# Scores of a prompt attention as float32r products over split keys, in place of float32 products over padded rows

## What is computed

```python
for l in range(DEPTH):
    fq, fk, fv, flf, mq, mckv, mkpe, sq, sk, sv = _mixer_inputs(_rmsnorm(xp, g_attn[l]), pos_p, *proj)
    o_a = _sweep(fq, fk, fv, True, jnp.cumsum(flf, axis=1))
    mk, mv = _mla_kv(mckv, mkpe, w_ukv[l])
    o_b = _sweep(mq, mk, mv, False)
    o_c = _swa_prompt(sq, sk, sv, rel_bias, swa_sinks[l])
    xp = xp + _merge(o_a, o_b, o_c, w_out[l])
    xp = xp + _mlp(_rmsnorm(xp, g_mlp[l]), w_up[l], w_down[l])
# in each attention: logits = jnp.einsum('bqhd,bkhd->bhqk', q, k) * scale, then softmax, then the product with v
```

## Time and profile before

| | |
|---|---|
| median of 3 runs | 2810.1 us (2809.98 to 2814.61) |
| profiled execution | 2807.96 us, span 2806.0 us |
| mean granted clock of PE | 0.989 |
| PE busy | 2695.5 us, 96% |
| DVE, ACT, POOL busy | 1698.6, 1054.8, 1050.4 us (61, 38, 37%) |
| chain that ended last | PE 86%, DVE 8%, ACT 2%, issue 2% |

### The profile page before, as it was taken

One profiled execution on the slowest core, in us unless ns is written; L12 is line 12 of the kernel. 1 busy time (PEld: TensorE's weight loads), 2 busy tenths in 40 slices (PEclk: granted clock), 3 DMA queues, 4 the chain that ended last, 5 costly groups with the idle time before them and its releaser, 6 DMA issues.

```text
span 2806.0 us, 39617 instructions
## 1 busy us (share of the span) xinstructions
PE 2695.5 (96%) x14966; PEld 2177.9 (78%) x14966; DVE 1698.6 (61%) x2196; ACT 1054.8 (38%) x1969; POOL 1050.4 (37%) x594
## 2 busy tenths in 40 slices
PE   8999999899999999999999999998999999999997
PEld 6986666787888887888879756667878888878886
DVE  4026777635564558778740377775355564688777
ACT  4225544423323332333332255554243233333333
POOL 1112000114545457767511210001146444667766
PEclk9999999999999999999999999999999999999999
DMA  4212001432333446444132200013413433654441
GB/s 145 63 29 61 25 18 44 137 135 98 124 139 126 150 173 251 142 138 134 61 115 64 66 24 17 17 50 131 163 70 139 157 118 140 238 195 143 143 142 75
DMA packets 164722, 308.75 MB, mean 110 GB/s; under 512 B 24720, under 2 KB 90416, under 8 KB 164592
## 3 DMA queue, kind: packets, MB, share of 16 engines
q1 hardware_dynamic: 161280, 303.59, 31.4%
q10 hardware_dynamic: 3312, 3.41, 0.4%
HBM read 207.40 MB, written 97.72 MB: 109 GB/s over the span
## 4 chain that ended last, share of the span: by engine, by line
PE 86%; DVE 8%; ACT 2%; issue 2%; POOL 1%; DMA 1%; SPq 0%; DVEq 0%; ACTq 0%; POOLq 0%
PE ps L2583 8%; PE ps L2587 8%; PE ps L2585 8%; PE ps L2493 7%; PE ps L2494 7%; PE ps L2495 7%; PE ps L2237 6%; PE ps L2104 6%; PE ps L2106 6%; PE ps L2105 6%; PE ps L2098 5%; PE ps L2310 3%; PE ps L2370 2%; PE ps L2204 1%; PE ps L2438 1%
## 5 line engine op out<-in xcount | busy, mean ns | idle before, releaser
L2583 PE MATMUL ps<-wq_hi,sa_hi 128*128 128x512 f32 x896 | 349.0, 390 | 5.3 <-DVE x L2034 5.3
L2587 PE MATMUL ps<-wq_hi,sa_lo 128*128 128x512 f32 x896 | 348.6, 389 | 0.0
L2585 PE MATMUL ps<-wq_lo,sa_hi 128*128 128x512 f32 x896 | 348.6, 389 | 0.0
L2034 DVE TENSOR_TENSOR x<-ps,x 128x1024 f32<-128x1024 f32 x224 | 266.7, 1215 | 119.5 <-PE ps L2587 115.4
L1082 POOL TENSOR_TENSOR wq_lo<-wsum,wq_hi 128x1024 fp32r<-128x1024 f32 x64 | 157.5, 2462 | 289.7 <-ACT wq_hi L1454 289.7
L1972 DVE TENSOR_TENSOR sa_lo<-ra,sa_hi 128x1024 fp32r<-128x1024 f32 x112 | 253.3, 2263 | 19.8 <-ACT sa_hi L1474 19.7
L2104 PE MATMUL ps<-w_hi,hT_hi 128*128 128x512 f32 (+2 forms) x672 | 248.1, 369 | 0.3 <-DVE hT_lo L1643 0.3
L2106 PE MATMUL ps<-w_hi,hT_lo 128*128 128x512 f32 (+2 forms) x672 | 246.1, 366 | 0.0
L2105 PE MATMUL ps<-w_lo,hT_hi 128*128 128x512 f32 (+2 forms) x672 | 245.1, 365 | 0.0
L1964 DVE TENSOR_TENSOR cq<-ps,cq 128x1024 f32<-128x1024 f32 x48 | 58.6, 1221 | 285.4 <-ACT cq L1515 243.2
L2493 PE MATMUL ps<-hT_hi,wq_hi 128*128 128x512 f32 x512 | 203.2, 397 | 7.6 <-DVE hT_lo L1928 7.6
(11 more groups left out here) (323 smaller groups left out, 6188.1 us busy)
## 6 DMA issues: line engine op xcount, KB each, us to landing
ra<-hidden_scratch SPq DMA_DIRECT2D x112, 512.0 KB, 3.3
hidden_scratch<-cq SPq DMA_DIRECT2D x94, 512.0 KB, 2.7
rq<-in_w_up_dram SPq DMA_DIRECT2D x64, 512.0 KB, 3.9
rq<-in_w_down_dram SPq DMA_DIRECT2D x64, 512.0 KB, 4.3
residual_scratch<-x SPq DMA_DIRECT2D x27, 512.0 KB, 3.1
x<-residual_scratch SPq DMA_DIRECT2D x27, 512.0 KB, 7.3
x<-in_x_prompt_dram SPq DMA_DIRECT2D x16, 512.0 KB, 6.9
w_raw<-in_w_in_dram SPq DMA_DIRECT2D x16, 512.0 KB, 4.2
```

Of the source, the lines that this page charges most:

```text
L2034: nc.vector.tensor_tensor(part, bank(b0 + 2 * pair, 2).rearrange("p (t n) -> p t n", t=2), part, ALU.add).then_inc(dn_ev.sem, 1)
L2583: pe.matmul(out, ah[:, k, :], bh[:, k * 512:(k + 1) * 512], start=new and k == 0, stop=False, skip_group_check=True)
L2585: pe.matmul(out, ah[:, k, :], bl[:, k * 512:(k + 1) * 512], start=False, stop=False, skip_group_check=True)
L2587: last = pe.matmul(out, al[:, k, :], bh[:, k * 512:(k + 1) * 512], start=False, stop=final and k == 1, skip_group_check=True)
```

## The change

Each query and key of the prompt is split in a high part, rounded to float32r, and the rest. For every head the high parts of the 64 key rows lie in partitions 0 to 63 and the low parts in 64 to 127 (`keysF`, `keysS`), and the queries lie twice, one copy in each half. The scores are then two float32r products over all 128 rows, one with the queries' high part, one with their low part: q_hi by (k_hi + k_lo), then q_lo by (k_hi + k_lo).

DVE's `stg_copy` casts the high part from PSUM and subtracts to get the low one, into two pairs of buffers (`split_hi`, `split_lo`); it first waits until the stores of the tile two before have landed (signals `split_stored0`, `split_stored1`). The streams' tile is copied to `newF` and `newS` after all stores of its kind. A new function on ACT, `store_split(kind, t)`, issues six DMAs per tile: two that store the queries to DRAM and four that move 64 key rows across partitions. SP loads the queries of a tile from DRAM with two DMAs (one for each half of the partitions) into one buffer per kind, once the scores of the tile before are done. POOL's padding is gone, and the low parts of pieces 6 and 7 move one step ahead on DVE. Some buffers change their address; five semaphores of the final normalisation are replaced by others. Line numbers shift: 1223 becomes 1217, 1186 becomes 1180, 1653 and 1655 become 1685 and 1686, 1704, 1706 and 1716 become 1735, 1737 and 1747.

```diff
-        qkTf = at("qkTf", Z, [P, 4, TOK])
+        keysF = at("keysF", Z, [P, FOX_H, NPT * P])
+        newF = at("newF", Z + 16384, [P, 4, P])
         Vf = at("Vf", Z + 18432, [P, NT, 256])
-        qkTs = at("qkTs", Z + 27648, [P, 3, TOK])
+        keysS = at("keysS", Z + 27648, [P, 2, NPT * P])
+        newS = at("newS", Z + 39936, [P, 3, P])
         hbuf = [at(f"hbuf{i}", Z + 18432 + i * 4096, [P, D]) for i in range(2)]
...
-        qzf = [at(f"qzf{i}", (RING + 47104, HT + 71296)[i], [P, FOX_H, P]) for i in range(2)]
-        qzs = [at(f"qzs{i}", NRM + 8192 + i * 2048, [P, SWA_H, P]) for i in range(2)]
+        queriesF = at("queriesF", Z + 35840, [P, 2, 2, 2, P])
+        queriesS = at("queriesS", NRM + 8192, [P, 2, 2, 2, P])
...
+                def load_queries(kind, t):
+                    dst = queriesF if kind == "fox" else queriesS
+                    for half in range(2):
+                        load(dst[64 * half:64 * half + 64].rearrange("p r s k n -> p r (s k n)"),
+                             query_d[kind][t].rearrange("(r p) s n -> p r (s n)", r=2), queries_in[kind])
+
+                for i in range(2):
+                    sp.wait_ge(split_out[i].sem, split_out[i].at(l, 2 * SPLIT_TILES))
+                load_queries("fox", 0)
                 sp.wait_ge(kpe_ev.sem, kpe_ev.at(l, NPT))
                 load(kTm[64:96, 1:MLA_H, :], kTm[64:96, 0:1, :].broadcast_to([ROPE, MLA_H - 1, NPT * P]), kpe_all)
+                sp.wait_ge(lat_ev.sem, lat_ev.at(l, NT))
+                sp.wait_ge(prep_out.sem, prep_out.at(l, 16 * 10))
+                load_queries("swa", 0)
                 for t in range(NPT - 1):
+                    for kind in ("fox", "swa"):
+                        sp.wait_ge(sc_mm.sem, sc_mm.at(l, scores_behind(kind, t)))
+                        load_queries(kind, t + 1)
                     sp.wait_ge(o_ev.sem, o_ev.at(l, TILE_END[t]))
...
-                def pad_queries(dst, src, planes, t):
-                    for r in range(2):
-                        rows = slice(64 * r, 64 * r + 64)
-                        last = nc.gpsimd.tensor_copy(dst[t % 2][rows, planes(r), :], src[rows, 0:2, toks[t]])
-                    last.then_inc(qz_ok.sem, 1)
...
+                def store_split(kind, t):
+                    m = t if kind == "fox" else NT + t
+                    act.wait_ge(stg_ev.sem, stg_ev.at(l, m + 1))
+                    if kind == "swa" and t < 2:
+                        for i in range(2):
+                            act.wait_ge(split_out[i].sem, split_out[i].at(l, SPLIT_TILES))
+                    done = split_out[t % 2]
+                    for j in range(2):
+                        part = (split_hi, split_lo)[j][kind][t % 2]
+                        act.dma_start(query_d[kind][t, :, j, :], part[:, 0:2, :].rearrange("p k n -> p (k n)").bitcast(F32)
+                                      ).then_inc(done.sem, 16)
+                        for r in range(2):
+                            rows, half = slice(64 * r, 64 * r + 64), slice(64 * j, 64 * j + 64)
+                            if kind == "fox":
+                                act.dma_start(keysF[half, r:FOX_H:2, toks[t]], part[rows, 2:4, :].bitcast(F32)).then_inc(done.sem, 16)
+                            else:
+                                act.dma_start(keysS[half, r, toks[t]], part[rows, 2, :].bitcast(F32)).then_inc(done.sem, 16)
...
+                    if t >= 4:
+                        store_split("fox", t - 4)
...
+                    if s == 1:
+                        store_split("fox", 5)
                     in_hi(4 * s + 2)
+                    if s == 1:
+                        store_split("fox", 6)
                     in_hi(4 * s + 3)
+                    if s == 1:
+                        store_split("fox", 7)
                     for t in range(NT):
                         if s < 3 and t in (3, 5):
                             in_hi(4 * s + 4 + (t == 5))
                         evac_z(s * NT + t)
+                        if s == 3 and t >= 3:
+                            store_split("swa", t - 3)
...
+                store_split("swa", 6)
+                store_split("swa", 7)
...
                 def stg_copy(m):
                     dve.wait_ge(stg_tp.sem, stg_tp.at(l, m + 1))
                     src = bank(6 + m % 2).rearrange("p (k n) -> p k n", k=4)
-                    if m < NT:
-                        nc.vector.tensor_copy(qkTf[:, :, toks[m]], src).then_inc(stg_ev.sem, 1)
-                    else:
-                        nc.vector.tensor_copy(qkTs[:, :, toks[m - NT]], src[:, 0:3, :]).then_inc(stg_ev.sem, 1)
+                    kind, t, planes, new = ("fox", m, 4, newF) if m < NT else ("swa", m - NT, 3, newS)
+                    if t == NPT:
+                        for i in range(2):
+                            dve.wait_ge(split_out[i].sem, split_out[i].at(l, SPLIT_TILES * (1 if m < NT else 2)))
+                        nc.vector.tensor_copy(new[:], src[:, 0:planes, :]).then_inc(stg_ev.sem, 1)
+                        return
+                    if t >= 2:
+                        dve.wait_ge(split_out[t % 2].sem, split_out[t % 2].at(l, splits_stored(kind, t - 2)))
+                    high, low = split_hi[kind][t % 2][:], split_lo[kind][t % 2][:]
+                    chain.link(nc.vector.tensor_copy(high, src[:, 0:planes, :]))
+                    nc.vector.tensor_tensor(low, src[:, 0:planes, :], high, ALU.subtract).then_inc(stg_ev.sem, 1)
...
                         if t == 2:
                             dve.wait_ge(skew_out.sem, 16)
-                        if t == NT + 1:
+                        if t == NT:
                             lo(6, 0, 2 * SLABS_IN[1][1])
                             lo(7, 1, 2 * SLABS_IN[1][1])
                         stg_copy(t - 2)
...
-                    if kind == "fox" and h0 == 0:
-                        pe.wait_ge(qz_ok.sem, qz_ok.at(l, t + 1 if t < 2 else 2 * t + 1))
-                    if kind == "swa" and h0 == 0:
-                        pe.wait_ge(qz_ok.sem, qz_ok.at(l, t + 3 if t < 2 else 2 * t + 2))
+                    if kind != "mla" and h0 == 0:
+                        if t == 0:
+                            for i in range(2):
+                                pe.wait_ge(split_out[i].sem, split_out[i].at(l, splits_stored(kind, NPT - 1)))
+                        pe.wait_ge(queries_in[kind].sem, queries_in[kind].at(l, 32 * (t + 1)))
                     for g in range(heads):
                         h, s0 = h0 + g, score_column(kind, t, g)
                         if kind == "fox":
-                            q, keys, mask = qzf[t % 2][:, h, :], qkTf[:, 2 + h // 2, :], cmaskB
+                            qs, keys = [queriesF[:, h % 2, j, h // 2, :].bitcast(F32R) for j in range(2)], keysF[:, h, :].bitcast(F32R)
                         elif kind == "swa":
-                            q, keys, mask = qzs[t % 2][:, h, :], qkTs[:, 2, :], None
+                            qs, keys = [queriesS[:, h // 2, j, h % 2, :].bitcast(F32R) for j in range(2)], keysS[:, h // 2, :].bitcast(F32R)
                         else:
-                            q, keys, mask = qTm[t % 2][:, h, :], kTm[:, h, :], None
+                            qs, keys = [qTm[t % 2][:, h, :]], kTm[:, h, :]
                         for c0 in range(0, w, 512):
                             c1 = min(w, c0 + 512)
-                            masked = mask is not None and c1 == w
+                            masked = kind == "fox" and c1 == w
                             out = S[:, s0:s0 + w]
-                            last = pe.matmul(out[:, c0:c1], q, keys[:, k0 + c0:k0 + c1], start=True, stop=not masked)
+                            for j, q in enumerate(qs):
+                                last = pe.matmul(out[:, c0:c1], q, keys[:, k0 + c0:k0 + c1], start=(j == 0),
+                                                 stop=(j == len(qs) - 1 and not masked))
                             if masked:
-                                last = pe.matmul(out[:, w - P:w], identB[:], mask[:], start=False, stop=True)
+                                last = pe.matmul(out[:, w - P:w], identB[:], cmaskB[:], start=False, stop=True)
                     last.then_inc(sc_mm.sem, 1)
```

More of the change, by code:

```diff
@@ L175 @@
 ACT_CHAIN, POOL_CHAIN = 1, 2 * NT + 1
-DVE_CHAIN = 8 + 2 * NT + (NATTN + 2 * NSWA) + (2 * NI + 4)
+DVE_CHAIN = 8 + 2 * NPT + 2 * NT + (NATTN + 2 * NSWA) + (2 * NI + 4)
+SPLIT_TILES = 16 * 6 * NPT // 2
 SCALE64 = HD ** -0.5
@@ L283, in hybrid_step @@
         stg3 = [at(f"stg3_{i}", RING + 32768 + i * 2048, [P, 512]) for i in range(2)]
+        split_hi = {"fox": [at(f"splitF_hi{i}", Z + (31744, 16384)[i], [P, 4, P], F32R) for i in range(2)],
+                    "swa": [at(f"splitS_hi{i}", LATT + i * 3072, [P, 3, P], F32R) for i in range(2)]}
+        split_lo = {"fox": [at(f"splitF_lo{i}", Z + (33792, 73728)[i], [P, 4, P], F32R) for i in range(2)],
```

(21 more changed lines are left out.)

44 lines of the change are left out of this document (9 added, 35 removed).

## The result

| | before | with the change |
|---|---|---|
| median | 2812.36 us (4 runs) | 2852.92 us (2847.64 to 2856.15, 4 runs) |
| profiled span | 2806.0 us | 2850.4 us |
| mean granted clock of PE | 0.989 | 0.979 |

The kernel is slower by 40 us: ratio 1.0142 (95% interval 1.0122 to 1.0162). The forecast, 2823 with a range to 2841, had the sign and too small a size.

A forecast was written before the change was run, and what follows sets the result against it. Attention was taken as PE and DVE taking turns, with stores delaying the projection. Per layer -10 + 1 + 6.5 + 9 = +6.5 us; two layers +13 on 2810.1 gave 2823 us, range 2798 to 2841.

The forecast's parts named there:

- the tail: End of slab 3: tile 7's copy waits for tile 5's stores, so latT starts late; +9 us per layer (5.7 to 12).
- slab 0: Projection's first slab: ACT's idle time hides the issues, DVE's wait for landings not wholly; +1 us per layer (0 to 3).
- the seam: Slab 0 to slab 1: store issues stand ahead of ACT's weight casts and PE waits; +6.5 us per layer (4 to 9).
- the scores: Prompt attention: cheaper float32r products, -10 us per layer (bounds -7 and -20.2), half of the 20.2 if PE never waited.
- rival 1: Attention: PE alone sets the pace, all 20.2 us per layer gained; with cheap stores 2790 us; chance 0.12.
- The bound of 13.9: Attention: DVE's reductions wait 13.9 us per layer for scores, the most gain that DVE's own order lets through.
- Price of an issue: ACT's store issues: six per tile cost 2.0 to 2.7 us, taken as 2.6.
- The landing: Tail's stores: the skill's nearly constant 2.0 us per transfer would make the tail lose 6.0 us in place of 9.
- Rival 3: Whole layer: dear stores and DVE-bound attention, -7 + 3 + 9 + 12 = +17 us per layer, 2844 us; chance 0.10.
- Rival 4: Seam and tail: low clock after each new long PE wait adds 5 us per layer, 2833 us; chance 0.08.
- Rival 2: Whole layer: cheap issues and landings, middle attention gain; -0.3 us per layer, 2810 us, no change; chance 0.20.
- Rival 5: Attention: scores get no cheaper, two float32r products cost one float32; +16.5 us per layer, 2843 us; chance 0.05.

The follow-up runs named there:

- e3: The kernel before, with forgetting and sliding scores as two float32r products over the old padded buffers, no stores or query loads: 2798.6 us, ratio 0.9950.
- e9: e3 with one float32r product per score in place of two: 2804.7 us, ratio 0.9970 to the kernel before.
- e1: The change with every store set issued one step earlier, six issues per tile kept: 2825.4 us, ratio 1.0039 to the kernel before.
- e8: The change with SP's loads and stores of the tail issued only after all the tail's store sets landed: 2846.0 us, ratio 1.0127 to before.

## Why the prediction was right and wrong

By the marks the two layers lost 20.3 and 22.4 us where the sum had 6.5. Of the difference the tail makes 6.3 and 7.2, slab 0 2.6 and 5.7, the seam 2.0 in each and the scores 2.9 and 1.0.

- **Scores, -10 per layer forecast: right in mechanism, somewhat high.** The stage gained 7.1 and 9.0 us by the marks, e3's 8.0 and 8.1, and e9 shows that PE alone (rival 1) was not the pace. The bound of 13.9 from DVE's waits held; half of 20.2 was a little too much.
- **Price of an issue: the step that failed first.** I took 0.43 us, from SP's rows and ACT's single 0.338, six for 2.6. ACT's issues back to back, after, over the whole run:

```profile
L1254 ACTq DMA_DIRECT2D keysF<-splitF_hi x32: 603/623/713, 49.6 to 1509.9; - x32
```

  A forgetting set is 3.7 us, a sliding one 3.3 to 3.5, that of tile 7 5.4. A lone issue was the wrong row for six in a row. Why SP's five were cheaper, by the queue or by what they move, no run shows.
- **Slab 0, +1 (0 to 3): too small.** 3.6 in layer 0 and 6.7 in layer 1, by the start of PE's wait at the seam. I counted the landing for the copy and left it there; the low part of the next tile stands behind the copy on DVE, and PE waits for that one. e1 took the wait away, not the issues, and slab 0 fell to 2.3 and 2.8.
- **The seam, +6.5 (4 to 9): near.** 8.5 in each layer: two waits of 4.49 and 2.88 in place of 0.78, and some 1.6 of work lost to the clock (5 us at 0.68, from 95 to 100). The mechanism is the forecast's, the price of the set made the rest.
- **The tail, +9 (5.7 to 12): the largest miss.** 15.3 and 16.2. The landing of tile 5's set was forecast at 9 us after the last product and came at 10, in part by luck: six issues of 3.5 us and a landing of 6.0 stood in for one store held for 8.0. But I let the streams' copy, which waits for tile 7's set, come "at about the same moment". That set was issued only after tile 7's copy, its six issues took 5.4 us (up to 1.35 each) beside SP's own, and it landed 10.7 us after tile 7's copy began; the three pairs of latents that should have covered it were done in 2 us. Two waits in a row were costed as one.
- **The landing.** The Trainium skill (DMA: Bandwidth & Descriptors, section "Anatomy of one DMA — SWDGE (gpsimd) path") has a nearly constant 2.0 us, in a section on transfers that GpSimd issues. The landings of ACT's moves in slab 0, from 48 to 54 us, agree (2.0 to 2.1 for L1254). Those of L1256 in the tail, from 214 to 218 us, do not, and the tail lost 15.3, not the 6.0 that the prediction worked out from that figure:

```profile
DMA to landing us min/median/max: 3.2/4.9/6.0
```

- **The rivals.** Rival 3 (all stores dear, +17 per layer) was the nearest in total, 2844, and in mechanism: what it needed, copies held by landings, is what slab 0 and the tail show. Its -7 for the scores and +9 for the seam are near; +3 for slab 0 and +12 for the tail were still too small. Rival 4's mechanism took part in the seam alone: in the tail PE works at half clock from 235.3 to 241.5 us after as it did from 207.9 to 214.1 before. The windows, after and before:

```profile
235.30:241.50 6.20, 6.19 (x33) 6.20 (x34) 4.01 (x8) 0.93 (x4) 2.08 (x2) 0.50 0.25 85
...
207.90:214.10 6.20, 6.20 (x33) 6.20 (x34) 3.99 (x8) 0.95 (x4) 2.08 (x2) 0.50 0.51 127
```

  Rivals 1, 2 and 5 fell. Rival 5's total, 2843, was as near as rival 3's, but by luck: its condition is false, since the scores did get cheaper.

What stays open: how far SP's transfers alone, without its issues, hold the tail's landings, since e8 moved both; and what lowers the clock behind the faster attention.

## What to carry to other kernels

A store that frees a buffer is part of the loop of the engine that fills that buffer: ask in which step it is issued, whether it lands before the same engine's next turn, and what is queued behind the waiting instruction. One step earlier was worth 27 us here; fewer issues, spread between evacuations, and buffers outside the region that the next stage needs first made the same idea 0.57% faster instead of 1.4% slower. And price a run of issues by a run of issues on that queue, not by a lone one.

## What was not expected of the hardware

A DMA issue on ACT behind another mostly took 0.60 to 0.63 us in the forgetting sets, nearly twice a lone one (0.338); the stores of L1249, of one shape, took 0.44 in the median at the head of a set and 0.61 behind two moves. While SP issued too (224 to 230 us), two moves took 2.71 on ACT; with SP quiet, in e8, such a pair took 1.1. SP's two stores beside them, 2.52, were no dearer by it: before, with no issue on ACT near, they took 2.35.

```profile
212.11 2.35 SPq L661 DMA_DIRECT2D out_dram<-Vs  x2
```
